# One stage for gate products and memory attention over blocks of 256 tokens, with gating, division and splitting moved to the output stage

## The chip, the core and the metric

The kernel runs on one core of a Trainium2 chip. The metric is the time of the device in microseconds (us), the median of several executions. One further execution was recorded by the hardware profiler; all rows shown here come from it. The engines are TensorE (PE: products, with PEld its weight loads), VectorE (DVE), ScalarE (ACT), GpSimd (POOL) and SyncE (SP), which in this kernel issues every DMA on one queue. Each engine works through its own instructions in order, and they meet at semaphores.

## The reference

Two request groups of 2048 and 512 tokens (2560 rows of width 1024) go through two layers with the same weights. Layer 0 mixes by latent attention with 12 heads, layer 1 by a spatial gating MLP. Both have a memory attention beside it and a gate on top. Cut to what the change touches:

```
q = rmsnorm(q_mem.reshape(S, 4, 64), mq_g)               # q_mem, gate: columns of h @ w_in
s = einsum('qhd,khd->hqk', q, k) * 64 ** -0.5            # k, v: 256 memory rows
o_mem = einsum('hqk,khd->qhd', softmax(s), v)            # 256 columns
o = concatenate([o_mix, o_mem]) * silu(gate)             # o_mix: 768 columns
x = x + o @ w_out[i]
```

All in float32. The kernel keeps that precision by splitting each factor into a high part and a low part and by making three products (hi x hi, hi x lo, lo x hi) of each.

## The kernel before

The program is a sequence of stages. Each has its own buffers and semaphores (`Space`) and ends in a barrier of all engines: `latents`, `heads`, `attention`, then for each layer (`spatial` first in layer 1) `memory_keys` (names mk_), `memory_attention` (ma_), `gating` (ga_) and `output` (ou_). Between stages data lies in DRAM: `hT` (normed input, transposed and split, 1 MB for each of 20 tiles of 128 tokens), `omix` (o_mix and o_mem, transposed), `sums` and `inv_s` (softmax sums of the 12 heads and their reciprocals, since layer 0's o_mix isn't divided yet), `ogT` (gated o, transposed and split).

**Weights.** A `Plan` lists the tiles of a stage's weights. One raw buffer of 6144 columns is shared by all stages; as many tiles as fit (8 at most) are loaded in the stage before (`load_following`, line 137), after that stage has split its own. ACT rounds each tile to its high part (`round_hi`, line 149), DVE takes the low part (`take_lo`, line 154), SP loads the others as slots come free (`load_rest`, line 131). PE waits for single tiles (`ready`).

**attention.** SP loads q of chunk 0, K of head 0, q of chunk 1, V of head 0, q of chunk 2, then K and V of head 1, and then `row(c0)` (line 1006): four small copies of the negated maxima of chunk 0 into a row of q, without which PE can't make the first scores (line 1077). They wait for `neg_in`, which DVE raises after the maxima of all of head 0's keys.

**memory_attention** (line 1432) goes through 20 tiles of 128 tokens with each engine's order staggered over four tiles. For one tile: PE makes q (24 products of 256 columns), ACT squares it, DVE sums over heads, POOL raises the mean to -1/2, DVE scales, PE turns q, ACT and DVE round and split it, PE makes scores (6 products of 512 columns), DVE takes the maximum and its scaled negative `ntop`, ACT makes four exponentials with their sums, DVE divides, PE turns p (8 transposes), ACT and DVE round and split, PE makes the values (16 products of 128 columns), ACT and DVE add the two halves, SP stores to `omix`.

**gating** (line 1668) goes through 5 blocks of 512 tokens by 8 groups of 128 gate columns, 24 products of 512 columns each (960 in all), four PSUM buffers deep. ACT takes silu, DVE divides o (layer 0: the first 6 of the 8 groups, by `inv_s`), multiplies, ACT and DVE split, SP stores `ogT` in two DMAs a group, and loads h, o and the reciprocals. In layer 0 DVE first adds the two rows of `sums` and takes the reciprocal (lines 1800 and 1802).

**output** (line 1828) goes through 20 tiles: load o, split already (1 MB), 48 products of 512 columns, DVE adds x (line 1899), SP stores. ACT does nothing but round the weights. With the last tiles of a stage SP has already fetched the next stage's weights: in layer 0 those are the spatial stage's, 4 x 0.75 MB.

Of the kernel before, what the change touches and what calls it, by code (L numbers as in the profile page):

```python
# [12 lines left out]
P = 128  # L13
# [915 lines left out]
def attention(nc, K, qT, kT, vS, omix, sums_out):  # L929
# [4 lines left out]
    with Space(nc, "at") as s:  # L934
# [52 lines left out]
        with nc.Block() as block:  # L987

            @block.sync
            def _(sp):  # L990
# [441 lines left out]
def memory_attention(nc, K, plan, following, g_q, hT, M, omix, name):  # L1432


    SC = float(MHD) ** -0.5
    with Space(nc, name) as s:
        w = Weights(s, plan, following)
        h = s.sb("h", [P, 2, 2, D], F32R)
# [11 lines left out]
        e = s.sb("e", [P, MH, MEM])  # L1450
        pn = s.sb("pn", [P, 2, MH, MEM])
        p_hi = s.sb("p_hi", [P, MH * 2, P], F32R)
        p_lo = s.sb("p_lo", [P, MH * 2, P], F32R)
        up = s.sb("up", [MHD, MH * P])
        ost = s.sb("ost", [MHD, 2, MH * P])
        q_ps = s.ps("q", [P, MW])
        t_ps = s.ps("t", [P, 2, P])
        s_ps = s.ps("s", [P, MH, MEM])
        p_ps = s.ps("p", [P, MH * 2, P])
        o_ps = s.ps("o", [P, MH * P])  # L1460
        (g_in, mm, squared, red, mean_in, rstd_in, normed, turned, qh, ql, scored, top_in, ntop_in, exps,
         inv_in, pn_in, p_turned, ph, plo, valued, up_in, o_in) = (s.sem(n) for n in (
             "g_in", "mm", "squared", "red", "mean_in", "rstd_in", "normed", "turned", "qh", "ql", "scored",
             "top_in", "ntop_in", "exps", "inv_in", "pn_in", "p_turned", "ph", "plo", "valued", "up_in",
             "o_in"))
        h_in = [s.sem(f"h{u}") for u in range(2)]
        o_out = [s.sem(f"o_out{u}") for u in range(2)]
        with nc.Block() as block:

            @block.sync  # L1470
            def _(sp):
                sp.dma_start(g[:], g_q).then_inc(g_in, 16)
                for u in range(2):
                    sp.dma_start(f32(h[:, u]), hT[u]).then_inc(h_in[u], 16)
                w.load(sp)

                def step(j, u):
                    t, t2, t3 = Tile(j, u), Tile(j, u, 2), Tile(j, u, -3)
                    if t2.within(TILES):
                        sp.wait_ge(mm, t.n + 1)  # L1480
                        sp.dma_start(f32(h[:, u]), hT[bass.ds(t2.n, 1)].rearrange("o p a n -> (o p) a n")
                                     ).then_inc(h_in[u], 16)
                    if t3.within(TILES):
                        sp.wait_ge(o_in, t3.n + 1)
                        sp.dma_start(omix[MIX:MIX + MW, bass.ds(t3.n * P, P)].rearrange(
                            "(h d) t -> d h t", h=MH),
                            ost[:, t3.slot, :].rearrange("d (h t) -> d h t", h=MH)
                            ).then_inc(o_out[t3.slot], 16)

                run_tiles(sp, 3, step, 3)  # L1490
                for u in range(2):
                    sp.wait_ge(o_out[u], 16 * TILES // 2)

            @block.tensor
            def _(pe):
                def q_of(t):
                    pe.wait_ge(h_in[t.slot], t.half * 16 + 16)
                    after(pe, normed, t.n)
                    for k in range(KD):
                        if t.known and t.n == 0:  # L1500
                            w.ready(pe, "q", k)
                        ks = slice(k * P, (k + 1) * P)
                        m = product(pe, q_ps[:], h[:, t.slot, 0, ks], h[:, t.slot, 1, ks],
                                    w.hi["q"][:, k], w.lo["q"][:, k], k == 0, k == KD - 1)
                    m.then_inc(mm, 1)
# [40 lines left out]
                def step(j, u):  # L1546
                    for what, t in ((turn_p, Tile(j, u, -3)), (turn_q, Tile(j, u, -1)),
                                    (q_of, Tile(j, u)), (values, Tile(j, u, -3)),
                                    (scores, Tile(j, u, -1))):
                        if t.within(TILES):  # L1550
                            what(t)
# [692 lines left out]
```

## Time and profile before

| | us |
|---|---|
| median of 3 executions (lowest, highest) | 3594.59 (3593.68, 3597.07) |
| the profiled execution | 3603.56 |
| its span, first to last instruction | 3601.5 |

| engine | busy us | share of the span |
|---|---|---|
| PE | 3326.9 | 92% |
| PEld | 2735.6 | 76% |
| DVE | 2006.2 | 56% |
| ACT | 1581.8 | 44% |
| POOL | 1389.1 | 39% |

The mean granted clock of TensorE is 0.951 of full speed.

| stretch of the span | stage |
|---|---|
| 497 to 1746 | attention |
| 1746 to 1787 | memory_keys, layer 0 |
| 1787 to 1963 | memory_attention, layer 0 |
| 1963 to 2208 | gating, layer 0 |
| 2208 to 2437 | output, layer 0 |
| 2437 to 2910 | spatial |
| 2910 to 2951 | memory_keys, layer 1 |
| 2951 to 3371 | memory_attention and gating, layer 1 |
| 3371 to 3601 | output, layer 1 |

Some durations of single instructions that occur again after the change, from the groups by line: silu of 128x512 0.60, DVE's subtraction of 128x1024 1.22, its addition from PSUM of 128x1024 1.23, ACT's rounding of 128x1024 1.04, addition and reciprocal of the sums 0.40 and 1.65, table load of ACT 1.28.

How to read the rows: each instruction has a start, a duration, an engine, a line, and names of what it writes and reads. What stands in brackets is the time that its engine stood idle before it, and who ended that. A row of PE gives the latency of a product; consecutive products overlap, so what a run of them costs is the distance of starts. A row of SP gives the time that issuing took. Rows with "x4" are several instructions in one.

### The profile page before, as it was taken

Reading aid. Unit: us, or ns where it says so; the run is one execution under the profiler, and the core shown is the slowest. Engines: PE = TensorE matmul, PEld = TensorE weight load, DVE = VectorE, ACT = ScalarE, POOL = GpSimd, SP = SyncE. Lnnn points to the kernel's source line nnn. Section 1 sums busy time; section 2 is a strip of 40 time slices with the busy share of each in tenths; the row PEclk is TensorE's granted clock in tenths of the full one; section 3 lists DMA queues with packets and bytes.
Section 4 is the critical chain, followed back from the end, with each engine's and each line's share of the span. In section 5 each row is a group of like instructions: output and inputs, shape, how many; then the busy total and the mean of one; then the engine's idle time right before and its main releaser. Section 6 shows DMA issues by size and latency. Waiting matters only on the chain. (4 is left out here: it accounts for less than half of the span.)

```text
span 3601.5 us, 46116 instructions
## 1 busy us (share of the span) xinstructions
PE 3326.9 (92%) x16108; PEld 2735.6 (76%) x16108; DVE 2006.2 (56%) x3007; ACT 1581.8 (44%) x2396; POOL 1389.1 (39%) x914
## 2 busy tenths in 40 slices
PE   8969959999999999999697998997999959799899
PEld 8968837777777777777496887885888849688787
DVE  4457758888888888888376332113333337522211
ACT  4446627777777777777454121003222225412100
POOL 1148828888888888888410000000000011000000
PEclk9979969999999999999898999998999969799999
DMA  7769980222222221221354996554222244488555
GB/s 279 260 225 314 306 233 18 66 67 61 67 62 65 52 56 44 67 61 22 115 174 129 290 292 217 197 175 177 88 91 103 90 180 165 131 259 242 175 189 173
DMA packets 454870, 537.91 MB, mean 149 GB/s; under 512 B 55609, under 2 KB 372409, under 8 KB 434993
## 3 DMA queue, kind: packets, MB, share of 16 engines
q1 hardware_dynamic: 454704, 535.81, 48.5%
q8 instruction: 92, 1.51, 0.2%
q14 instruction: 74, 0.60, 0.1%
HBM read 324.98 MB, written 210.61 MB: 149 GB/s over the span
## 5 line engine op out<-in xcount | busy, mean ns | idle before, releaser
L1235 POOL TENSOR_TENSOR at_acc<-at_acc,at_ph 128x1024 f32<-128x1024 f32 x288 | 690.9, 2399 | 79.0 <-ACT at_ph L1161 58.2
L1269 DVE TENSOR_TENSOR at_pl<-at_sc,at_ph 128x1024 fp32r<-128x1024 f32 x408 | 498.6, 1222 | 139.3 <-ACT at_sc L1162 139.0
L1161 ACT ACTIVATE at_ph<-at_sc 128x1024 fp32r<-128x1024 f32 x408 | 418.5, 1026 | 336.2 <-PE at_sc L1081 336.1
L1255 DVE TENSOR_REDUCE at_mx<-at_mxp 128x1 f32<-128x512 f32 x816 | 522.2, 681 | 26.7 <-PE at_mxp L1092 25.0
L1162 ACT ACTIVATE at_sc<-at_sc 128x1024 f32<-128x1024 f32 x408 | 416.3, 1020 | 0.0
L1077 PE MATMUL at_sc<-at_qt,at_kt 97*128 97x512 f32 x816 | 331.4, 406 | 12.5 <-DMA at_qt<-at_neg 9.7
L1079 PE MATMUL at_sc<-at_qt,at_kt 96*128 96x512 f32 x816 | 326.0, 399 | 0.0
L1106 PE MATMUL at_o_hi<-at_ph,at_v 128*128 128x512 f32 x816 | 322.4, 395 | 2.1 <-DVE at_half L1274 2.1
L1081 PE MATMUL at_sc<-at_qt,at_kt 96*128 96x512 f32 x816 | 323.7, 397 | 0.0
L1108 PE MATMUL at_o_lo<-at_pl,at_v 128*97 128x512 f32 x816 | 321.8, 394 | 0.0
L1092 PE MATMUL at_mxp<-at_kt,at_qt 96*128 96x512 f32 x816 | 276.8, 412 | 25.2 <-DMA at_kt<-kT 20.4
L165 PE MATMUL ga_acc<-ga_h,ga_g_hi 128*128 128x512 f32 x640 | 256.1, 400 | 28.4 <-DMA ga_h<-hT 27.6
L165 PE MATMUL ou_acc<-ou_o_hi,ou_o 128*128 128x512 f32 x640 | 250.8, 392 | 26.2 <-DMA ou_o<-ogT 26.2
L1899 DVE TENSOR_TENSOR ou_y<-ou_acc,ou_x 128x1024 f32<-128x1024 f32 x40 | 49.0, 1225 | 380.9 <-PE ou_acc L167 380.9
L166 PE MATMUL ga_acc<-ga_h,ga_g_hi 128*128 128x512 f32 x640 | 253.4, 396 | 0.0
L167 PE MATMUL ga_acc<-ga_h,ga_g_lo 128*128 128x512 f32 x640 | 253.3, 396 | 0.0
L166 PE MATMUL ou_acc<-ou_o_lo,ou_o 128*128 128x512 f32 x640 | 250.5, 391 | 0.0
L167 PE MATMUL ou_acc<-ou_o_hi,ou_o 128*128 128x512 f32 x640 | 250.2, 391 | 0.0
L1092 PEld LDWEIGHTS at_mxp<-at_kt,at_qt 96*128 96x128 f32 x816 | 156.3, 192 | 91.5 <-DVE at_mx L1255 33.0
L253 POOL TENSOR_TENSOR sg_n_mse<-sg_n_ms,all_eps 128x1 f32<-128x1 f32 x24 | 5.0, 209 | 560.0 <-ACT sg_n_junk L245 560.0
L1077 PEld LDWEIGHTS at_sc<-at_qt,at_kt 97*128 97x128 f32 x816 | 154.5, 189 | 75.6 <-DVE at_pl L1269 26.8
L165 PE MATMUL sg_acc<-sg_uv_hi,sg_n_h 128*128 128x512 f32 x480 | 194.6, 406 | 1.8 <-ACT sg_uv L2022 1.2
(246 smaller groups left out, 7350.5 us busy)
## 6 DMA issues: line engine op xcount, KB each, us to landing
ma_h<-hT SPq DMA_DIRECT2D x40, 1024.0 KB, 4.8
ogT<-ga_st SPq DMA_DIRECT2D x160, 256.0 KB, 3.5
ou_o<-ogT SPq DMA_DIRECT2D x40, 1024.0 KB, 6.1
ga_h<-hT SPq DMA_DIRECT2D x64, 512.0 KB, 7.3
hT<-lat_n_h SPq DMA_DIRECT2D x24, 1024.0 KB, 6.2
hT<-sg_n_h SPq DMA_DIRECT2D x24, 1024.0 KB, 3.8
qT<-hd_stq SPq DMA_DIRECT2D x60, 384.0 KB, 6.2
kT<-hd_stk SPq DMA_DIRECT2D x120, 192.0 KB, 3.5
```

Of the source, the lines that this page charges most:

```text
L165: pe.matmul(out, a_hi, w_hi, start=first, stop=False)
L166: pe.matmul(out, a_hi, w_lo, start=False, stop=False)
L167: return pe.matmul(out, a_lo, w_hi, start=False, stop=last)
L1077: pe.matmul(sc[g][:, b, :], kt[:, c.kv, 0, ks], qt[:, c.quad, 0, :], start=True, stop=False)
L1079: pe.matmul(sc[g][:, b, :], kt[0:QK, c.kv, 0, ks], qt[0:QK, c.quad, 1, :], start=False, stop=False)
L1081: m = pe.matmul(sc[g][:, b, :], kt[0:QK, c.kv, 1, ks], qt[0:QK, c.quad, 0, :], start=False, stop=True)
L1092: pe.matmul(mxp[n % 2][:], qt[0:QK, c.quad, 0, qn * P:(qn + 1) * P], kt[0:QK, c.kv, 0, kb * BLK:(kb + 1) * BLK], start=True, stop=True).th ...
L1161: act.activation(ph[:, g], sc[g % 2][:], ACT.Exp, scale=SCALE).then_inc(p_hi, 1)
L1162: act.activation(sc[g % 2][:], sc[g % 2][:], ACT.Exp, scale=SCALE).then_inc(p_in, 1)
L1235: pool.tensor_tensor(acc[:, c.slot, :], f32(ph[:, (g - 1) % 4]).rearrange("p b n -> p (b n)") if t == 1 else acc[:, c.slot, :], now, ALU.a ...
L1255: dve.tensor_reduce(mx[:, n:n + 1], mxp[n % 2][:], AX.X, ALU.max).then_inc(mx_in, 1)
L1269: dve.tensor_tensor(pl[:, g], sc[g % 2][:], f32(ph[:, g]), ALU.subtract).then_inc(p_lo, 1)
```

## The change

- `memory_attention` and `gating` become one stage, `gate_memory` (names gm). It goes through 10 blocks of 256 tokens. For each of the two tiles of a block the steps of memory attention are made as before (two exponential buffers, no buffer for divided p), and the 8 groups of gate products, now 256 columns wide, stand between them in an order written out by hand. The values are made for both tiles at once, 16 products of 256 columns. ACT takes silu of two groups at a time (128x512, four a block), and SP stores it to a new array `sgT` in one DMA. Loops are unrolled.
- h is loaded by blocks (2 MB), two buffers deep, once; gating's own loading of h is gone, and so are its loading of o and its storing of `ogT`.
- Weights: q's eight tiles are laid into two of 128x1024 (`Spaced`), with gate's eight in one plan of ten. Six fit in the raw buffer and are fetched in `memory_keys`.
- In layer 0 the sums are loaded after h of blocks 0 and 1; DVE adds and inverts them ahead of its first norm.
- `gated_output` loads `omix`, `sgT` and, in layer 0, the reciprocals repeated to 64 partitions, in pieces of 128 tokens (512 bytes); DVE divides (768 columns) and multiplies (1024), ACT rounds, DVE takes the low part, PE multiplies with the weights as before. The first tile's steps stand ahead of the rounding and splitting of weights on ACT and DVE, and DVE prepares tile i + 1 ahead of the addition of tile i.
- In `attention` `row(c0)` moves ahead of the loads of chunk 2's q and of head 1's K and V.

The diff, cut to its core:

```diff
@@ attention, sync
                 load_v(0)
+                sp.wait_ge(const_in, 5)
+                row(c0)
                 load_q(c0.ahead(2))
                 load_k(1)
                 load_v(1)
-                sp.wait_ge(const_in, 5)
-                row(c0)
@@ gate_memory (was memory_attention and gating)
+                load_h(0)
+                w.load_rest(sp)
+                load_h(1)
+                if sums is not None:
+                    sp.dma_start(rows[:], flat).then_inc(rows_in, 16)
+                w.load_following(sp)
...
+                def step(b):                       # tensor
+                    i = TB * b
+                    q_of(i)
+                    gates(b, 0)
+                    turn_q(i)
+                    q_of(i + 1)
+                    scores(i)
+                    gates(b, 1)
+                    turn_q(i + 1)
+                    gates(b, 2)
+                    scores(i + 1)
+                    turn_p(i)
+                    gates(b, 3)
+                    gates(b, 4)
+                    turn_p(i + 1)
+                    gates(b, 5)
+                    values(b, 0)
+                    gates(b, 6)
+                    values(b, 1)
+                    gates(b, 7)
...
+                def exp(i):                        # scalar
+                    act.wait_ge(ntop_in, i + 1)
+                    after(act, p_turned, i - 1)
+                    after(act, inv_in, i)
...
+                def step(b):                       # scalar
+                    i = TB * b
+                    square(i)
+                    q_round(i)
+                    square(i + 1)
+                    exp(i)
+                    silu(b, 0)
+                    q_round(i + 1)
+                    p_round(i)
+                    exp(i + 1)
+                    silu(b, 1)
+                    p_round(i + 1)
+                    silu(b, 2)
+                    upper(b, 0)
+                    upper(b, 1)
+                    silu(b, 3)
...
+                def step(b):                       # vector
+                    i = TB * b
+                    norm(i)
+                    norm_scale(i)
+                    q_low(i)
+                    norm(i + 1)
+                    maximum(i)
+                    norm_scale(i + 1)
+                    divide(i)
+                    q_low(i + 1)
+                    maximum(i + 1)
+                    p_low(i)
+                    divide(i + 1)
+                    p_low(i + 1)
+                    halves(b, 0)
+                    halves(b, 1)
@@ gated_output (was output), sync
-                sp.dma_start(f32(o[:, 0]), ogT[0]).then_inc(o_in[0], 16)
+                load_o(0)
                 w.load_rest(sp)
-                sp.dma_start(f32(o[:, 1]), ogT[1]).then_inc(o_in[1], 16)
+                load_o(1)
                 for u in range(2):
                     sp.dma_start(x[:, u, :], rows_of(u)).then_inc(x_in[u], 16)
                 w.load_following(sp)
+                for i in range(TILES):
+                    u = i % 2
+                    if i + 2 < TILES:
+                        sp.wait_ge(mixed, i + 1)
+                        load_o(i + 2)
@@ gated_output, scalar and vector
+                round_og(0)
                 w.round_hi(act)
+                for i in range(1, TILES):
+                    round_og(i)
...
+                gated(0)
+                low(0)
+                w.take_lo(dve)
+                for i in range(TILES):
+                    if i + 1 < TILES:
+                        gated(i + 1)
+                        low(i + 1)
+                    add(i)
@@ build
-                      Plan(raw, [("q", k_tiles(w_in, q0, q0 + MW), MW)]),
-                      Plan(raw, [("g", k_tiles(w_in, q0 + MW, q0 + MW + D), D)]),
+                      Plan(raw, [("q", Spaced(w_in, q0).rows, D),
+                                 ("g", k_tiles(w_in, q0 + MW, q0 + MW + D), D)]),
```

Step names: `gates(b, f)` is one group of 24 gate products (G0 to G7), `turn_q`, `scores`, `turn_p`, `values` are PE's steps of memory attention for tile i, `divide` and `halves` DVE's.

## Rows read from the trace of the kernel before

**Rows 1.** Busy time by stretch: us, each engine's busy time, PEclk, DMA share, GB/s.
```profile
1787.40:1963.20 175.80, 153.73 (x1120) 144.98 (x1120) 119.75 (x268) 84.84 (x249) 20.14 (x20) 0.91 0.43 153
1963.20:2207.70 244.50, 226.10 (x960) 182.93 (x960) 82.86 (x120) 54.48 (x89) 0.00 (x0) 0.95 0.93 266
2020.00:2100.00 80.00, 80.00 (x354) 66.25 (x353) 29.35 (x45) 18.16 (x32) 0.00 (x0) 1.00 1.04 295
2951.10:3371.50 420.40, 380.87 (x2080) 328.96 (x2080) 181.02 (x356) 139.91 (x339) 20.14 (x20) 0.93 0.66 199
```

**Rows 2.** Timeline of PE, one tile of memory attention: start us, us, engine, line, operation.
```profile
1903.46 0.23 PE L1540 MATMUL ma_o<-ma_p_hi,mem_mv 128*128 128x128 f32 x1
...
1905.20 0.45 PE L165 MATMUL ma_s<-mem_mk_hi,ma_qT_hi 128*128 128x512 f32 x1
...
1906.65 1.04 PE L1529 MATMUL ma_p<-all_ident,ma_pn 128*128 128x128 f32 x8
...
1907.53 0.38 PE L1511 MATMUL ma_t<-all_ident,ma_qn 128*128 128x128 f32 x2
...
1907.66 0.36 PE L165 MATMUL ma_q<-ma_q_hi,ma_h 128*128 128x256 f32 x1
...
1910.61 0.23 PE L1540 MATMUL ma_o<-ma_p_hi,mem_mv 128*128 128x128 f32 x1
```

**Rows 3.** Timeline at the start of attention, and four copies later (603.16).
```profile
499.66 13.46 SPq L992 DMA_DIRECT2D at_qt<-qT  x1
...
520.87 11.10 SPq L1009 DMA_DIRECT2D at_qt<-at_neg  x4
...
534.18 0.80 PE L1077 MATMUL at_sc<-at_qt,at_kt 97*128 97x512 f32 x1 [9.74 <-DMA at_qt<-at_neg]
...
603.16 2.42 SPq L1009 DMA_DIRECT2D at_qt<-at_neg  x4
```

**Rows 4.** Timeline of the first tile of memory attention: q's square and its turning.
```profile
1797.67 0.38 ACT L1589 ACTIVATE ma_sq<-ma_q 128x256 f32<-128x256 f32 x1 [7.67 <-PE ma_q L167]
...
1800.39 0.69 PE L1511 MATMUL ma_t<-all_ident,ma_qn 128*128 128x128 f32 x2 [2.81 <-DVE ma_qn L1646]
```

**Rows 5.** Timeline of ACT and DVE in a steady tile of memory attention.
```profile
1900.17 1.21 DVE L1613 TENSOR_REDUCE ma_top<-ma_s 128x4 f32<-128x1024 f32 x1
...
1900.57 1.01 ACT L1572 CAST ma_p_hi<-ma_p 128x1024 fp32r<-128x1024 f32 x1 [1.75 <-PE ma_p L1529]
...
1901.85 0.48 ACT L1583 ACTIVATE ma_e<-ma_s,ma_ntop 128x256 f32<-128x256 f32 x1
...
1903.66 0.40 ACT L1589 ACTIVATE ma_sq<-ma_q 128x256 f32<-128x256 f32 x1
...
1904.03 1.14 DVE L1633 TENSOR_SCALAR ma_pn<-ma_e,ma_inv 128x256 f32<-128x256 f32 x4
```

**Rows 6.** Timeline of layer 1 where its first exponential needs another table.
```profile
2972.57 1.28 ACT L1583 ACT_TABLE_LOAD   x1
...
2972.71 0.17 DVE L1616 TENSOR_SCALAR ma_ntop<-ma_top 128x4 f32<-128x4 f32 x1
...
2973.86 0.47 ACT L1583 ACTIVATE ma_e<-ma_s,ma_ntop 128x256 f32<-128x256 f32 x1
```

**Rows 7.** Timeline at the starts of memory attention, gating, output and memory_keys.
```profile
1759.10 0.33 SPq L1334 DMA_DIRECT2D mk_h<-hT  x1
...
1792.72 0.58 PE L165 MATMUL ma_q<-ma_q_hi,ma_h 128*128 128x256 f32 x1 [9.39 <-DMA ma_h<-hT]
...
1964.26 6.90 DVE L154 TENSOR_TENSOR ga_g_lo<-all_w_raw,ga_g_hi 128x1024 fp32r<-128x1024 f32 x6 [4.56 <-ACT ga_g_hi L149]
...
2212.77 0.80 PE L165 MATMUL ou_acc<-ou_o_hi,ou_o 128*128 128x512 f32 x1 [13.10 <-DMA ou_o<-ogT]
```

**Rows 8.** Timeline at the end of gating.
```profile
2201.00 1.46 DVE L1807 TENSOR_TENSOR ga_st<-ga_og,ga_st 128x512 fp32r<-128x512 f32 x2
```

**Rows 9.** DMA issues of attention's V: KB each, median us to landing.
```profile
at_v<-vS SPq DMA_DIRECT2D x12, 1280.0 KB, 7.8
```

More of the change, by code:

```diff
@@ new lines, in q_of, with gates @@
+                    m.then_inc(q_mm, 1)
+                def gates(b, f):
+                    m = b * PAIRS + f // 2
+                    if f % 2 == 0:
+                        after(pe, sg_in, m - 1)
+                    fs = slice(f * P, (f + 1) * P)
+                    for k in range(KD):
+                        if b == 0 and f == 0:
+                            w.ready(pe, "g", k)
+                        ks = slice(k * P, (k + 1) * P)
+                        last = product(pe, gate[m % 2][:, f % 2, :], w.hi["g"][:, k, fs], w.lo["g"][:, k, fs],
+                                       h[:, b % 2, :, 0, ks], h[:, b % 2, :, 1, ks], k == 0, k == KD - 1)
+                    if f % 2 == 1:
+                        last.then_inc(gate_mm, 1)
@@ L1546, in step, with values @@
[L1546 to L1551, printed above, removed]
-                run_tiles(pe, 3, step, 3)
+                def values(b, half):
+                    group = TB * b // PT_TILES
+                    if half == 0:
+                        pe.wait_ge(plo, TB * (b + 1))
+                    after(pe, o_in, 2 * b + half)
+                    for n in range(2 * half, 2 * half + 2):
+                        out = ot[:, (n % 2) * W:(n % 2 + 1) * W]
+                        for c in range(2):
+                            vt = M.v[:, group, c, n].rearrange("p a d -> p (a d)")
+                            pe.matmul(out, vt, p_hi[:, 2 * n + c, :], start=c == 0, stop=False)
+                            m = pe.matmul(out, vt, p_lo[:, 2 * n + c, :], start=False, stop=c == 1)
+                    m.then_inc(valued, 1)
@@ L1867, in _ @@
             def _(pe):
-                def step(j, u, first, last):
-                    i = j * 2 + u
-                    pe.wait_ge(o_in[u], j * 16 + 16)
-                    if not first:
-                        pe.wait_ge(y_in, i - 1)
+                for i in range(TILES):
+                    u = i % 2
+                    pe.wait_ge(lo_in, i + 1)
+                    after(pe, y_in, i - 1)
                     for k in range(KD):
-                        if first and u == 0:
+                        if i == 0:
                             w.ready(pe, "o", k)
@@ L1890, in _, with gated @@
             def _(dve):
[L1891 to L1894 removed]
+                def gated(i):
+                    u = i % 2
+                    dve.wait_ge(o_in[u], LOADS * (i // 2 + 1))
+                    if inv_s is not None:
+                        dve.tensor_tensor(o[:, u, 0:DIV], o[:, u, 0:DIV], r[:, u], ALU.mult
+                                          ).then_inc(divided, 1)
+                        dve.wait_ge(divided, i + 1)
+                    after(dve, lo_in, i)
+                    dve.tensor_tensor(full[:], o[:, u].rearrange("p k t -> p (k t)"),
+                                      sg[:, u].rearrange("p k t -> p (k t)"), ALU.mult).then_inc(mixed, 1)
```

498 lines of the change are left out of this document (194 added, 304 removed).

## The prediction

> **What bounds the kernel now.** I read four views in this order: the engines' busy shares and the slices of the page, busy time by stretch, the order of instructions in time inside each stage that the diff touches, and the groups by line. TensorE is busy 92% of the span. In the middle of a stage it never stops: 80 us of gating hold 80.00 us of PE and 354 products at the full clock, 0.226 us each [rows 1]. What is left over sits at the ends of stages, where the engine waits and its granted clock falls: memory attention plus gating take 420.3 us in the first layer and 420.4 us in the second, at a granted clock of 0.91 to 0.95 [rows 1].
>
> Inside them the steady part is small. One tile of memory attention lasts 7.16 us: q 2.95, values 1.74, scores 1.45, turning p 0.88, turning q 0.13 [rows 2]. Twenty tiles are 143 us, and 960 gate products at 0.2266 are 217.5 us, together 360.7. So 59.6 us per layer are start, drain and barriers of two stages, which one stage can partly save.
>
> **The sum is made against the profiled execution**, 3603.56 us with a span of 3601.5. It lies 9.0 us above the median 3594.59, and I take 9.0 off at the end.
>
> **Part 1: attention's first row.** SP's fifth load is held 13.46 us at issue, behind the queue's earlier loads [rows 3]. The next K and V go out behind it, and then the four small copies of the maxima take 11.10 us to issue, where the same four take 2.42 us in a quiet queue; PE waits 9.74 us for them until 534.18 [rows 3]. After the change nothing is issued between the first V load and these copies. They start at 520.87 as before, since the maxima come no earlier, and are there at about 520.9 + 1.8 + 2.0 = 524.7. Gain 9.4. The second K and V then load beside chunk 0 and are used a head later; the third q a chunk later. Bounds: 5 (the queue is still half full) and 9.7.
>
> **Part 2: the joint stage, per block of two tiles.** PE's work, each from rows 2: q 48 products x 0.1195 = 5.7; scores 2.9; turning p 1.8; turning q 0.3. The gate product is now 256 columns wide. q's 256-column products take (2.95 - 0.08)/24 = 0.1195 us, and 512 columns take 0.2266, so halving costs 0.0124 us each: 192 x 0.1195 = 22.9 for what took 96 x 0.2266 = 21.8. The values go the other way, 16 products of 256 columns, 1.9, for 32 of 128 columns, 3.5. With about 0.8 for the changes of kind the sum is 36.3 us; before, two tiles took 14.3 + 21.8 = 36.1. The work itself is a tie.
>
> Then the waits. From q's end to q's turning the chain ACT, DVE, POOL, DVE takes 2.8 us [rows 4]; one gate group (24 x 0.1195 = 2.9) covers it, leaving 0.1. The second tile's chain is covered by scores and a group, 4.3.
> The long chain begins at q_of(i+1)'s end, set to 0. Scores end at 1.45, the maximum (1.21) and its scaling at 3.1 [rows 5]. Four exponentials, 1.81 [rows 5], end at 5.05. ACT must then change its table: the load is 1.28 us [rows 6]. Silu (0.60, like the other single durations without a group from the short list beside the tables of time and profile) ends at 6.95, q's rounding at 7.4, its low part at 7.95. PE reaches scores(i+1) at 7.45, so it stalls 0.5. Later, counted from that point C: p turned at 2.3, rounded (1.01) at 3.55, table load, exponentials at 6.65, divided (1.14 for four) at 8.05; PE arrives at turn_p(i+1) at 8.1. No stall. The rest, G5 to G7 and the two halves of the values, has gate groups of 2.9 between steps of 1.4. Block: 36.3 + 0.1 + 0.5 = about 36.8 (7.95 + 28.8 by the same walk). Ten blocks: 368, 7.3 more than the 360.7.
>
> Four table loads a block, 80 in all, are 103 us of ACT, but ACT needs only some 16 us of 36.8. The load before exp(i) costs nothing if it runs ahead of the wait: in layer 1 it began 0.14 us before the ntop scaling had even started, and the exponential followed at once (2972.57 + 1.28 = 2973.85, started 2973.86) [rows 6]. That instruction had one wait; here exp has three, so a load could stand behind the first of them (a rival below).
> The Trainium skill speaks against this part. Its page "ScalarE: Activation LUTs", section "What ACT_TABLE_LOAD costs", gives 1283 ns for the load and about 1380 ns of drain, 2.66 us a switch, and the section on table sets tells one to batch calls by set. The load's figure is in the trace; the drain isn't. By the row the block is 36.8, by the page about 39.5.
>
> **Start of the joint stage.** T is the barrier's end (1787.4). Before, q's first product started at T + 5.3, after 1 MB of h [rows 7]. Now the block's 2.1 MB must be in: at about 0.30 MB/us (295 GB/s in rows 1) and 1.5 to 2 latency, T + 9. Four of ten weight tiles (2.1 MB) follow h: the last at T + 15.5, rounded at 16.5 and split at 17.8 (DVE 1.15 a tile, from six in 6.90) [rows 7]. ACT and DVE take all ten before the first square, so turn_q(0) starts at T + 20. In layer 0 DVE also waits for the sums, which SP issues behind the second block's 2.1 MB: T + 23.3, then the addition and the reciprocal (0.40 and 1.65), turn_q(0) at T + 27.7. From there the rest of block 0 is 30.9 + 2 for the low clock, nine blocks are 331.2, silu to barrier 5.7 (DVE's last split ended at 2202.5, the next stage began at 2207.7) [rows 1, 8]. Layer 0: 397.5; layer 1: 389.8. Gain 22.8 and 30.6.
>
> **The stage before it.** memory_keys now fetches 6 x 0.5 MB ahead, not 8 x 0.125, and its third h goes out at 1759.10 [rows 7] behind what is left of them, about 1 MB: + 3.5 us per layer (0 to 5).
>
> **The output stage.** PE's products are unchanged, 48 x 0.2266 = 10.9 a tile. New per tile: DVE 0.95 + 1.22 + 1.22 beside the addition's 1.23 (128x1024), 4.6; ACT 1.0. Both fit. SP issues four more loads, 0.6 each as in the quiet queue [rows 3]. DMA: layer 0 reads 2816 pieces of 512 B. V's load is 2560 pieces of 512 B, landing in 7.8 us [rows 9]; less 2 latency that is 2.3 ns a piece. By gating's 295 GB/s it is 1.7. So 4.9 to 6.4 us, and 3.3 for x and y: 8 to 9.7 of 10.9. It just fits.
> The start doesn't. PE began 5.1 us after the barrier [rows 7], since the weights' split needs no data of the stage. Now the first split stands on DVE behind gated(0) and low(0), and ACT's rounding behind round_og(0): load 7.5, product 0.95 + 1.22, rounding 1.0, low 1.22, first split 1.2: PE at 13.3 in layer 0, + 8.2; in layer 1, with fewer pieces and no division, + 6.2. In layer 0 load_o(1) waits for two splits, which costs tile 1 about 2.5, and load_o(2) is queued behind the 3.1 MB of the spatial stage's weights: about 40.8 against the 35 at which tile 2 would need it, some 6 to 9 more (0 to 9). Output: + 19 in layer 0, + 6.5 in layer 1.
>
> **Sum.** Attention - 9.4; layer 0: - 22.8 + 3.5 + 19 = - 0.3; layer 1: - 30.6 + 3.5 + 6.5 = - 20.6. Together - 30.3: 3573.3 profiled, **3564.5 as a median**. Nearly all of the gain is in attention and in layer 1.
>
> **Rivals.**
> (a) The table load stands behind exp's first wait. Then exp(i) starts 1.3 later and so does scores(i+1): block 38.1, + 1.3 x 20 = 26: 3591. For: three waits. Against: the load that the trace shows ran ahead of its one.
> (b) A switch holds ACT for two loads' time, 2.57: scores(i+1) at 9.3 and turn_p(i+1) 1.2 late, block 39.3, + 2.5 x 20 = 50: 3615, slower. It decides from about 1.9 us a switch. Against: 0.01 us between load and exponential [rows 6]. This is the direction in which the skill's page above would take it.
> (c) Slower: the output stage becomes DMA-bound. The reads are columns of two arrays and rows repeated to 64 partitions. It decides where a piece costs over 2.7 ns (2816 x 2.7 + 3.3 = 10.9); at 3.5 ns a tile of layer 0 takes 13.1, 20 tiles + 44: 3609. For: V's 2.3 is near, and no repeated row of this size is in the trace. Against: gating moved 295 GB/s in such pieces.
> (d) More gain: the starts overlap better (keys + 0, no late load_o): 3548.
>
> **How the numbers follow.** Forecast 3564.5 within 12 us: 0.50; (d) 0.13; (a) 0.20; (b) 0.05; (c) 0.12. The 8-in-10 range reaches down to (d) with more of the first row's bounds and up past (a): 3540 to 3600. A measurement of this kernel can tell about 0.2%, 7.2 us. Faster by over that (below 3587.4): the forecast, (d) and a small part of (a), 0.66; within it: most of (a), 0.18; slower: (b), (c), 0.16.
>
> **What would show it.** Right: PE's first score product in attention near 525; blocks of 36.8 us in the joint stage with a stall of about 0.5 us before the second tile's scores and table loads directly after the previous ACT instruction; turn_q(0) 20 and 28 us after the barriers; PE in output starting 13 and 11 us after the barrier, then 10.9 us a tile. Wrong: blocks of 38 or more (then see where the load stands against exp's waits, and what lies between load and function), output tiles over 11 us that wait on DMA, or PE idle between later blocks, which would mean that an ordering of ACT or DVE which I walked through once does not repeat.

## The result, and the profile after

| | before | after |
|---|---|---|
| median of 4 executions (lowest, highest), us | 3595.83 (3593.68, 3597.61) | 3546.10 (3543.66, 3553.82) |
| span of the profiled execution, us | 3601.5 | 3546.5 |
| mean granted clock | 0.951 | 0.963 |

The ratio is 0.9864, 95% interval 0.9851 to 0.9877: by the medians the changed kernel is 49.7 us faster. Forecast was 30.3 less than before, 3564.5 us, with 3540 to 3600 as the range. The two traced executions lie further apart than the medians, 55.0 us, because that of before was 7.8 us above its median and that of after 2.3.

By stretch, in the columns of rows 1; the stretches are attention, memory_keys, the joint stage and output of layer 0, then 100 us from the middle of the joint stage, then the joint stage and output of layer 1:

```profile
494.53:1730.09 1235.56, 1208.06 (x5016) 919.46 (x5016) 1065.35 (x1409) 888.74 (x997) 1057.92 (x529) 0.98 0.25 58
1730.09:1775.13 45.04, 27.21 (x104) 21.18 (x104) 15.87 (x40) 12.64 (x32) 7.59 (x6) 0.80 0.44 163
1775.13:2163.22 388.09, 364.97 (x2880) 354.64 (x2880) 135.16 (x272) 170.49 (x329) 20.14 (x20) 0.97 0.30 103
2163.22:2412.25 249.03, 222.56 (x960) 182.92 (x960) 101.50 (x88) 28.78 (x28) 0.00 (x0) 0.95 0.77 216
1900.00:2000.00 100.00, 99.07 (x790) 96.34 (x790) 33.20 (x71) 43.78 (x88) 6.04 (x6) 1.00 0.29 98
2928.72:3309.96 381.24, 364.62 (x2880) 354.29 (x2880) 133.14 (x270) 171.78 (x330) 20.14 (x20) 0.98 0.30 104
3309.96:3546.40 236.44, 220.63 (x960) 181.83 (x960) 81.12 (x68) 28.79 (x28) 0.00 (x0) 0.96 0.62 182
```

The joint stage stands for two stages of before, 420.3 us together [rows 1]. Its clock is 0.97, theirs was 0.91 and 0.95. Stage by stage, in us:

| | before | after | difference | forecast |
|---|---|---|---|---|
| start to attention | 497.1 | 494.5 | -2.6 | 0 |
| attention | 1249.3 | 1235.6 | -13.7 | -9.4 |
| memory_keys, layers 0 and 1 | 41.1, 41.2 | 45.0, 43.4 | +4.0, +2.2 | +3.5, +3.5 |
| joint stage, layer 0 | 420.3 | 388.1 | -32.2 | -22.8 |
| output, layer 0 | 229.5 | 249.0 | +19.5 | +19 |
| spatial | 472.7 | 473.1 | +0.4 | 0 |
| joint stage, layer 1 | 420.3 | 381.2 | -39.1 | -30.6 |
| output, layer 1 | 230.0 | 236.5 | +6.5 | +6.5 |
| sum | | | -55.0 | -30.3 |

The code ahead of attention is the same in all kernels here, and it ends anywhere from 493.2 to 499.8 us in their traces; its 2.6 us are no effect of the change. Single stages scatter too. memory_keys took 40.7 to 41.5 us in the three traces that have it with memory attention and gating behind it (before and two experiments), and 42.6 to 47.9 us in the nine with the joint stage behind it and memory_keys as in the changed kernel. Their means are 44.2 in layer 0 and 44.8 in layer 1, so the +4.0 and +2.2 of the table stand for about +3.1 and +3.5. In the table's trace PE waits once for its third h, 2.97 us in layer 0 (line below) and 1.79 in layer 1; before it did not wait there.

**Attention's start.** The timeline of SP and PE after the change, which answers rows 3:

```profile
517.94 2.52 SPq L1009 DMA_DIRECT2D at_qt<-at_neg  x4
...
521.92 0.80 PE L1077 MATMUL at_sc<-at_qt,at_kt 97*128 97x512 f32 x1 [0.41 <-DMA at_qt<-at_neg]
...
523.37 0.63 PE L1077 MATMUL at_sc<-at_qt,at_kt 97*128 97x512 f32 x1
...
528.94 0.40 PE L1077 MATMUL at_sc<-at_qt,at_kt 97*128 97x512 f32 x1
```

The four copies take 2.52 us to issue instead of 11.10, and PE waits 0.41 us for them instead of 9.74. From the stage's first load to the first score it takes 27.4 us instead of 37.1. The scores run at 0.63 us until 526 and at 0.40 afterwards. The 0.63 us is not an effect of the wait alone: in both kernels the pairs of products for the maxima, which come before it, already took 1.39 us each, where later ones take 0.62.

**A block of the joint stage.** ACT, DVE and PE around the second tile's scores, answering rows 5 and 6:

```profile
1841.02 1.28 ACT L1667 ACT_TABLE_LOAD   x1
...
1843.27 0.17 DVE L1741 TENSOR_SCALAR gm_ntop<-gm_top 128x4 f32<-128x4 f32 x1
...
1843.47 0.47 ACT L1667 ACTIVATE gm_e<-gm_s,gm_ntop 128x256 f32<-128x256 f32 x1 [1.17 <-DVE gm_ntop L1741]
...
1845.42 1.28 ACT L1679 ACT_TABLE_LOAD   x1
...
1846.72 0.60 ACT L1679 ACTIVATE gm_sg<-gm_gate 128x512 f32<-128x512 f32 x1
...
1847.21 0.47 ACT L1660 ACTIVATE gm_qT_hi<-gm_ot,gm_g 128x256 fp32r<-128x256 f32 x1
...
1847.71 0.48 DVE L1733 SCALAR_TENSOR_TENSOR gm_qT_lo<-gm_ot,gm_g,gm_qT_hi 128x256 fp32r<-128x256 f32 x1 [0.92 <-ACT gm_qT_hi L1660]
...
1848.25 0.50 PE L165 MATMUL gm_s<-mem_mk_hi,gm_qT_hi 128*128 128x512 f32 x1 [0.31 <-DVE gm_qT_lo L1733]
```

Exp's table is loaded at 1841.02, 2.25 us before its `ntop` begins, and ACT then idles 1.17 us with the table in place. Silu starts 0.02 us after its load ends (1845.42 + 1.28 = 1846.70). The chain silu, rounding of q, low part ends last, and PE waits for it once a block. This is the path that the forecast walked. The distance of blocks is 36.39 to 36.42 us for all nine pairs in each layer. The groups by line count the loads of the stage, 79 in both layers together:

```profile
L1679 ACT ACT_TABLE_LOAD x40 | 51.3, 1283 | 0.7
L1667 ACT ACT_TABLE_LOAD x39 | 50.0, 1283 | 0.7
```

**The starts** of memory_keys and the joint stage (barrier T at 1775.13), and of the joint stage of layer 1 (T at 2928.72), by the timeline:

```profile
1750.97 0.50 PE L165 MATMUL mk_acc<-mk_kv_hi,mk_h 128*128 128x512 f32 x1 [2.97 <-DMA mk_h<-hT]
...
1782.23 0.49 SPq L1524 DMA_DIRECT2D gm_rows<-sums  x1
...
1794.78 0.41 DVE L1711 TENSOR_TENSOR gm_rows<-gm_rows 128x240 f32<-128x240 f32 x1 [3.36 <-DMA gm_rows<-sums]
...
1798.95 0.69 PE L1582 MATMUL gm_ot<-all_ident,gm_qn 128*128 128x128 f32 x2 [6.85 <-DVE gm_qn L1726]
...
2946.14 0.44 PE L1582 MATMUL gm_ot<-all_ident,gm_qn 128*128 128x128 f32 x2 [1.45 <-DVE gm_qn L1726]
```

Turning q(0) starts at T + 23.8 in layer 0, where DVE waited for the sums until 1794.78, and at T + 17.4 in layer 1.

**The output stage** (barriers at 2163.22 and 3309.96):

```profile
2171.13 0.96 DVE L1869 TENSOR_TENSOR ou_o<-ou_o,ou_r 128x768 f32<-128x768 f32 x1 [13.34 <-DMA ou_r<-inv_s]
...
2176.97 0.77 PE L165 MATMUL ou_acc<-ou_o_hi,ou_og 128*128 128x512 f32 x1 [17.65 <-DVE ou_o_lo L154]
...
2194.92 0.50 PE L165 MATMUL ou_acc<-ou_o_hi,ou_og 128*128 128x512 f32 x1 [4.34 <-DVE ou_og L1878]
...
2211.25 0.50 PE L165 MATMUL ou_acc<-ou_o_hi,ou_og 128*128 128x512 f32 x1 [3.52 <-DVE ou_og L1878]
...
3320.41 0.76 PE L165 MATMUL ou_acc<-ou_o_hi,ou_og 128*128 128x512 f32 x1 [14.30 <-DVE ou_o_lo L154]
```

PE starts 13.75 and 10.45 us after the barriers, where it was 5.1 before [rows 7]. Tiles 1 and 2 of layer 0 come late by 4.3 and 3.5 us, and then PE waits for nothing more in layer 0.

### The profile page after: what moved, and what is told of

It reads as the page before. It is cut to its first block and busy times, and to the rows that moved or that the text cites. A ratio compares the mean times of both kernels' runs of the same rounds, so it can differ in the third digit from the quotient of the medians.

```text
span 3546.5 us, 48006 instructions
## 1 busy us (share of the span) xinstructions
PE 3295.6 (93%) x17708; PEld 2787.6 (79%) x17708; DVE 2005.1 (57%) x2905; ACT 1686.6 (48%) x2420; POOL 1390.3 (39%) x914
## 5 line engine op out<-in xcount | busy, mean ns | idle before, releaser
L1255 DVE TENSOR_REDUCE at_mx<-at_mxp 128x1 f32<-128x512 f32 x816 | 521.7, 680 | 24.7 <-PE at_mxp L1092 23.1
L165 PE MATMUL gm_gate<-gm_h,gm_g_hi 128*128 128x256 f32 x1280 | 367.3, 287 | 1.8 <-DVE gm_g_lo L154 1.8
L166 PE MATMUL gm_gate<-gm_h,gm_g_hi 128*128 128x256 f32 x1280 | 362.1, 283 | 0.0
L167 PE MATMUL gm_gate<-gm_h,gm_g_lo 128*128 128x256 f32 x1280 | 362.0, 283 | 0.0
L1644 POOL TENSOR_TENSOR gm_rstd<-gm_mean,all_mhalf 128x4 f32<-128x4 f32 x40 | 40.3, 1007 | 681.3 <-DVE gm_mean L1721 681.3
L165 PE MATMUL ou_acc<-ou_o_hi,ou_og 128*128 128x512 f32 x640 | 252.3, 394 | 40.0 <-DVE ou_o_lo L154 32.0
L166 PE MATMUL ou_acc<-ou_o_lo,ou_og 128*128 128x512 f32 x640 | 251.8, 393 | 0.0
L167 PE MATMUL ou_acc<-ou_o_hi,ou_og 128*128 128x512 f32 x640 | 251.6, 393 | 0.0
L165 PEld LDWEIGHTS gm_gate<-gm_h,gm_g_hi 128*128 128x128 f32 x1280 | 244.8, 191 | 3.1 <-DVE gm_g_lo L154 2.2
L166 PEld LDWEIGHTS gm_gate<-gm_h,gm_g_hi 128*128 128x128 f32 x1280 | 245.1, 191 | 0.9
L167 PEld LDWEIGHTS gm_gate<-gm_h,gm_g_lo 128*128 128x128 f32 x1280 | 245.0, 191 | 0.0
```

The source lines that it names most:

```text
L165: pe.matmul(out, a_hi, w_hi, start=first, stop=False)
L166: pe.matmul(out, a_hi, w_lo, start=False, stop=False)
L167: return pe.matmul(out, a_lo, w_hi, start=False, stop=last)
L1255: dve.tensor_reduce(mx[:, n:n + 1], mxp[n % 2][:], AX.X, ALU.max).then_inc(mx_in, 1)
```

## Experiments

The theory after the result: each part does what the forecast said, and the sizes of the joint stage were off. What had to be told apart: whether the table loads are hidden, whether the 36.4 us of a block are work or waits, and what in the starts is late. All ratios are to the kernel before on the same chip; its median there was 3599.1 with the first four kernels, 3598.6 with the next four and 3598.2 with the last three. Differences to the changed kernel's 3546.1 cross these groups and are uncertain by some 8 us, so the stages of the traces are given beside them. "After" is the changed kernel.

**The row alone.** Before, with the two lines of the row moved:

```
+                sp.wait_ge(const_in, 5)
+                row(c0)
                 load_q(c0.ahead(2))
                 load_k(1)
                 load_v(1)
-                sp.wait_ge(const_in, 5)
-                row(c0)
```

> The kernel before with one edit: attention's row(c0) ahead of the loads of chunk 2's q and of head 1's K and V. Theory (the copies stood behind the V load in the queue, and TensorE's granted clock stayed low after the wait): attention shortens by 12 to 13 us, the first score product comes 9.7 us sooner after the stage's start, and the time is 3583. Rival (the row was worth only its wait, and the other 4 us of attention's gain came from something else in the change): 9.4 us, 3586.5.

3588.7 us, ratio 0.9972 (0.9962 to 0.9982): 10.1 us faster by the ratio, interval 6.5 to 13.7. The times allow both gains that were expected; the rival's, 9.3 below the 3595.8 of before, is nearer. The timeline of this kernel:

```profile
518.91 2.52 SPq L1009 DMA_DIRECT2D at_qt<-at_neg  x4
...
522.88 0.80 PE L1077 MATMUL at_sc<-at_qt,at_kt 97*128 97x512 f32 x1 [0.40 <-DMA at_qt<-at_neg]
```

**All but the row.** After, with the order of before in attention (the reverse of the diff above).

> The changed kernel with attention's order as before. Theory (the parts add up): 3546 + 12.5 = 3558.5. Rival (the row's move is worth less or more beside the others): outside 3554 to 3563.

3559.2 us, ratio 0.9888 (0.9871 to 0.9904). The wait is back:

```profile
522.96 9.77 SPq L1009 DMA_DIRECT2D at_qt<-at_neg  x4
...
536.01 0.79 PE L1077 MATMUL at_sc<-at_qt,at_kt 97*128 97x512 f32 x1 [9.48 <-DMA at_qt<-at_neg]
...
543.03 0.40 PE L1077 MATMUL at_sc<-at_qt,at_kt 97*128 97x512 f32 x1
```

The two parts add up within their intervals: by the ratios 40.3 us for the rest and 10.1 for the row, against 48.9 for both. The whole of attention took 1249.3, 1247.4 and 1244.2 us in the three traces with the old order (before, the split gates and this one) and 1235.1 to 1237.5 in ten traces with the new one. The means are 1247.0 and 1236.1: the row is worth 10.9, and the 13.7 of the first pair holds some 3 us of chance. Part of that chance is the clock. The kernel before, which waited 9.74 us, still ran scores at 0.63 us in this row:

```profile
546.11 0.63 PE L1081 MATMUL at_sc<-at_qt,at_kt 96*128 96x512 f32 x1
```

That is 11.9 us after its first score. The last such score came 8.5 us after the first in the kernel with gate products in halves (wait of 10.39 us), 4.9 us in this one (9.48 us), and 3.6 and 4.0 us in the two above that waited 0.4 us. Why the first stayed low for longest isn't settled.

**No table loads.** After, with silu replaced by a function that needs no other table. The product with the gate is then another function of it.

```
-  act.activation(sg[:, m % 2, :], gate[m % 2][:].rearrange("p f t -> p (f t)"), ACT.Silu
+  act.activation(sg[:, m % 2, :], gate[m % 2][:].rearrange("p f t -> p (f t)"), ACT.Square
```

> The changed kernel with Square in the place of Silu in gate_memory, a function for which no table has to be changed; silu is left out of what is computed. 80 table loads of 1.28 us, 103 us of ScalarE, are gone. Theory (they are hidden but for 0.3 us a block, where q's rounding of the second tile waits behind load and silu): 20 x 0.3 = 6 us less, 3540. Rival (a switch costs more than its load, or ScalarE sets the block): 25 us or more less, below 3521.

3533.9 us, ratio 0.9828 (0.9811 to 0.9844), 12.2 us below the changed kernel's median (13 by the ratios): twice what the theory had, half of the rival's least. The new function takes as long as silu, 0.60 us. Blocks went from 36.41 to 35.62 us (from one block's first q product to the next, 1873.86 to 1910.27 and 1871.62 to 1907.24). Below are 100 us of its stage and its second turning of p, where 0.12 us is the distance of products that wait for nothing:

```profile
1900.00:2000.00 100.00, 100.00 (x808) 98.22 (x807) 34.62 (x76) 30.80 (x81) 6.05 (x6) 1.00 0.29 100
```

```profile
1889.84 0.28 PE L167 MATMUL gm_gate<-gm_h,gm_g_lo 128*128 128x256 f32 x1
...
1889.96 1.03 PE L1600 MATMUL gm_p<-all_ident,gm_e 128*128 128x128 f32 x8
...
1890.76 0.36 PE L165 MATMUL gm_gate<-gm_h,gm_g_hi 128*128 128x256 f32 x1
```

In the changed kernel the same three rows are

```profile
1892.66 0.28 PE L167 MATMUL gm_gate<-gm_h,gm_g_lo 128*128 128x256 f32 x1
...
1892.92 1.09 PE L1600 MATMUL gm_p<-all_ident,gm_e 128*128 128x128 f32 x8
...
1893.77 0.36 PE L165 MATMUL gm_gate<-gm_h,gm_g_hi 128*128 128x256 f32 x1
```

So 79 loads of 1.28 us, 101 us of ACT, cost 12 or 13 us by the times and 15 by the blocks. They cost it in two places per block: 0.58 us between the last gate product and the second tile's first score product instead of 0.12, and 0.34 instead of 0.23 from that product to the next, 0.57 together; and 0.26 + 0.85 us around the second turning of p instead of 0.12 + 0.80, 0.19. Together 0.76.

**Gate products in halves.** Before, with each gating product of 512 columns made as two of 256:

```
-                    for k in range(KD):
+                    for c in range(2):
+                        cs = slice(c * BLK // 2, (c + 1) * BLK // 2)
+                        for k in range(KD):
...
-                        m = product(pe, acc[n % 4][:], w.hi["g"][:, k, fs], w.lo["g"][:, k, fs],
+                            m = product(pe, acc[n % 4][:, cs], w.hi["g"][:, k, fs], w.lo["g"][:, k, fs],
```

> The kernel before with each gate product of 512 columns made as two of 256, group by group, all k for one half and then for the other. 1920 more products in all. Theory (a product costs its columns and a fixed 0.0124 us): 1920 x 0.0124 = 24 us more, 3620. Rival (the width is free, and the changed kernel's blocks were short for another reason): within 5 us of 3596.

3627.9 us, ratio 1.0081 (1.0065 to 1.0098): 29 us slower (23 to 35), where 24 were expected; in its trace memory attention and gating together are 13.8 us longer in layer 0 and 15.0 in layer 1. The stretch of rows 1, in this kernel:

```profile
2020.00:2100.00 80.00, 80.00 (x669) 80.00 (x668) 26.57 (x41) 17.03 (x30) 0.00 (x0) 1.00 1.01 285
```

80 / 669 = 0.1196 us a product; the forecast had taken 0.1195 from the q products. Two of them are 0.239 where one of 512 columns is 0.226: 0.013 us each, 960 x 0.013 = 12.5 us a layer. So the narrower products cost what was expected. That the 0.013 us is a fixed cost of each product is not shown: by that rule 128 columns would take 0.066 us, and they take 1.74 / 16 = 0.109 [rows 2].

**Two switches more, at two places.** After, with two tiny activations (silu, exp) and so two more table loads a block, ahead of the first silu or ahead of the fourth:

```
+                def switches(b):
+                    for n, f in enumerate((ACT.Silu, ACT.Exp)):
+                        after(act, tiny_in, 2 * b + n)
+                        act.activation(tiny[:, n:n + 1], K.ones[:, 0:1], f).then_inc(tiny_in, 1)
...
+                    switches(b)
                     silu(b, 0)
```

> The changed kernel with two more table switches in each block, ahead of silu(b, 0): one Silu and one Exp of 128x1 into a spare tile, nothing else changed. Two loads and two small functions, about 3.1 us of ScalarE. Theory (this is the one place of the block where ScalarE is on TensorE's path): the block grows by 3.1, 20 x 3.1 = 62 us, 3608. Rival (ScalarE is busy only 16 of 36 us, so 3 more are covered): within 10 us of 3546.

> The same two small functions and two more table loads a block, but ahead of silu(b, 3), where ScalarE waits 2.3 us for the gate products and again 2.3 us before the next square. Theory: covered, 3546 within 8 us. Rival (each switch costs TensorE its own time wherever it stands, or drains more than it shows): 3596 or more.

Ahead of the first: 3637.2 us, ratio 1.0106 (1.0085 to 1.0128), 91 us above the changed kernel (87 by the ratios). Ahead of the fourth: 3550.1 us, 0.9864 (0.9843 to 0.9886); that this is the changed kernel's ratio to the last digit is chance, but its blocks take the same 36.4 us. The same 100 us in the kernel with them ahead of the fourth; ACT is busy 53.44 instead of 43.78, and PE is unmoved:

```profile
1900.00:2000.00 100.00, 99.05 (x789) 96.09 (x788) 33.87 (x75) 53.44 (x102) 6.05 (x6) 1.00 0.28 98
```

The other kernel, by its timeline in two neighbouring blocks and by the same stretch:

```profile
1855.57 0.50 PE L165 MATMUL gm_s<-mem_mk_hi,gm_qT_hi 128*128 128x512 f32 x1 [3.34 <-DVE gm_qT_lo L1741]
...
1857.08 1.88 PE L1602 MATMUL gm_p<-all_ident,gm_e 128*128 128x128 f32 x8
...
1896.42 0.50 PE L165 MATMUL gm_s<-mem_mk_hi,gm_qT_hi 128*128 128x512 f32 x1 [3.35 <-DVE gm_qT_lo L1741]
...
1897.93 1.03 PE L1602 MATMUL gm_p<-all_ident,gm_e 128*128 128x128 f32 x8
```

```profile
1900.00:2000.00 100.00, 93.31 (x730) 90.41 (x729) 29.44 (x61) 46.83 (x89) 4.04 (x4) 0.97 0.23 78
```

The wait grows by 3.03 us, the two loads and their two tiny functions. Blocks grow by 4.4 (40.84 instead of 36.4). I had expected 62 us more and got 91, because after a wait of 3.34 us the granted clock falls: in the first of the two blocks the eight transposes of p have a latency of 1.88 instead of 1.03 us, and the products behind them run at half speed until 1860.46. That is the other 1.4 us a block. It does not follow every time. In the second of the two blocks the wait is the same, the clock stays, and the block takes 39.46 us, 3.05 more than 36.41, which is the growth of the wait. Of the 18 distances of blocks in this trace two are of this kind, the others are 40.8 us or more. A load is free where ACT has slack, and costs more than its length where it is on the path.

**The output stage.** Two versions of after. In the first version the next stage's weights are fetched from tile 3 on, not ahead of tile 2:

```
-                w.load_following(sp)
                 for i in range(TILES):
...
+                    if i == 3:
+                        w.load_following(sp)
```

In the second also six weight tiles are rounded and split ahead of tile 0's gating, and `load_o(1)` goes out ahead of the stage's own last weights:

```
                 load_o(0)
-                w.load_rest(sp)
                 load_o(1)
+                w.load_rest(sp)
...
+                w.round_hi(act, 0, 6)
                 round_og(0)
-                w.round_hi(act)
+                w.round_hi(act, 6)
...
+                w.take_lo(dve, 0, 6)
                 gated(0)
                 low(0)
-                w.take_lo(dve)
+                w.take_lo(dve, 6)
```

> The changed kernel with the output stage's fetch of the next stage's weights (3.1 MB in layer 0) moved from ahead of tile 2's loads to behind tile 5's. Theory (tile 2's loads stand behind these weights in the queue, 3.52 us of wait, and the restart): 4 us less, 3542. Rival (tile 2 is late because its own pieces of 512 bytes are slow): 3546, and tile 2 still waits over 2 us.

> out_following, and in the output stage six of eight weight tiles are rounded and split ahead of tile 0's gating, tile 1's loads go out right behind tile 0's. Theory (the first split stands behind the data, and tile 1 behind all the splits): TensorE starts 1 us sooner in each layer, tile 1 isn't late in layer 0 (4.34 us), together with the above 10 to 12 us less than the changed kernel, 3535. Rival (the loads' bandwidth sets the start, so the order only moves the wait): less than 5 us beyond out_following.

The first: 3551.9 us (3545.6 to 3555.2), ratio 0.9867 (0.9849 to 0.9884), no difference that the times can tell. In its trace output of layer 0 takes 245.8 us, not 249.0, and tile 2's wait of 3.52 us is gone while tile 1's stays. The second: 3537.8 us, ratio 0.9828 (0.981 to 0.9846), 8.3 us below the changed kernel's median (13 by the ratios); the trace of the output stages is the surer measure here. Output of layer 0 takes 242.0 us, 7.1 less, and in layer 1 236.5, the same as after. Its starts:

```profile
2174.27 0.96 DVE L1871 TENSOR_TENSOR ou_o<-ou_o,ou_r 128x768 f32<-128x768 f32 x1 [2.09 <-DMA ou_r<-inv_s]
...
2178.88 0.80 PE L165 MATMUL ou_acc<-ou_o_hi,ou_og 128*128 128x512 f32 x1 [18.60 <-DVE ou_og L1880]
...
3315.78 0.80 PE L165 MATMUL ou_acc<-ou_o_hi,ou_og 128*128 128x512 f32 x1 [15.37 <-DVE ou_og L1880]
```

PE starts at T + 14.7 (T = 2164.18), later than the 13.75 of after, because tile 0's data now shares the DMA engines with tile 1's and lands at T + 10.1 instead of T + 7.9. The expected earlier start did not come. But no tile is late afterwards: the gain is the waits of tiles 1 and 2, 7.9 us, less the 0.9 of the later start.

**The swap, and everything together.** After again on the same chip; after with ScalarE's order changed in one place; and a version with all that the above pointed to.

```
                     exp(i)
-                    silu(b, 0)
                     q_round(i + 1)
+                    silu(b, 0)
```

The last one has this swap, the mended output stage (four weight tiles ahead of tile 0, the order of loads as in after), and three edits in the starts: `load_following` of memory_keys behind its last h; the sums fetched ahead of the second block's h, and added and inverted behind the first tile's low part of q; the first square ahead of ACT's last weight tile.

> The changed kernel as it is, beside the two others on one chip, so that their differences to it need no second chip. Expected: 3546 us (3540 to 3554), as in its first timing.

> The changed kernel with one swap in ScalarE's order per block: the rounding of the second tile's q stands ahead of the first silu instead of behind it. Nothing is added or removed, and the table loads stay as they are. Theory: the 0.76 us that a block is longer than the block without table loads all hangs on the one wait of 0.31 us of PE before scores(i+1), which ends with the low part of q, and that one with the rounding behind silu(b,0). With the swap the wait is gone and the block takes 35.6 instead of 36.4 us: 20 x 0.76 = 15 us less than the changed kernel, 3531. Rival: the other 0.45 us of the 0.76 come from ScalarE being slower elsewhere in the block (its groups freed later by the table loads), and only the 0.31 idle goes: 6 us less, 3540, with blocks of 36.1.

> The changed kernel with five orders mended: the next stage's weights fetched behind memory_keys' last h (6 us in both layers), the sums fetched ahead of the second block's h and added after the first q's low part (3 us in layer 0), the rounding of the second q ahead of silu(b,0) (15 us), the first square ahead of the last weight tile's rounding (1 us a layer), and in the output stage four weight tiles rounded and split ahead of the first tile's gating, with the next stage's weights fetched from tile 3 on (7 to 10 us in layer 0, 0 to 2 in layer 1). Sum by the theory: 3546 - 6 - 3 - 15 - 2 - 9 = 3511. Rival: these gains overlap other waits of the same starts, and only the swap's 15 us and the output's 7 are real: 3524.

After again: 3551.1 us, ratio 0.987 (0.9855 to 0.9885). The swap: 3539.0 us, 0.9839 (0.9826 to 0.9852), 12.1 less. Its block is 35.85 us (1871.98 to 1907.83), 0.56 less, between the two theories and explained by neither alone: the whole of the first place goes, the stall with its restart (0.57), and the second place stays. PE and ACT there:

```profile
1843.98 0.49 ACT L1660 ACTIVATE gm_qT_hi<-gm_ot,gm_g 128x256 fp32r<-128x256 f32 x1
...
1844.48 1.28 ACT L1679 ACT_TABLE_LOAD   x1
...
1845.78 0.60 ACT L1679 ACTIVATE gm_sg<-gm_gate 128x512 f32<-128x512 f32 x1
...
1846.48 0.39 PE L165 MATMUL gm_s<-mem_mk_hi,gm_qT_hi 128*128 128x512 f32 x1
```

All together: **3517.5 us (3514.2 to 3520.1), ratio 0.9775 (0.9761 to 0.9788)**, 80.7 us below before and 33.6 below after, where 3511 was expected. That sum had counted 35 from a median of 3546; on this chip the changed kernel stood at 3551.1, so the gain itself came out as expected. By its trace, memory_keys and the joint stage of layer 0 give 16.2 us (3.4 in memory_keys; turning q(0) at T + 18.6 instead of T + 23.8; 5.7 by the swap; most of the remaining 1.9 fits the second tile's q, which runs at 0.28 us from 1795.04 on, where in the changed kernel it ran at 0.41 us from 1799.65 to 1803.07), output of layer 0 7.9, and layer 1 from memory_keys to the end 7.7, where I had counted on 12. Layer 1's part is 1.8 in memory_keys, 4.6 in the joint stage and 1.3 in output. The joint stage has the swap's 5.7, but q(0) is turned at T + 18.6, 1.1 us later than in the changed kernel: PE's first product there waits for h until T + 8.9 instead of T + 7.9. That this comes from fetching the weights later is likely and not tested.

## Why the prediction was right and where it was off

The direction, the path and the parts were right; the forecast time was 18.4 us above the one measured. In the traces the difference to the forecast is 24.7 us. The joint stages of both layers are 9.4 and 8.5 us of it, 17.9 together, and attention and what stands ahead of it 6.9, mostly chance; the rest cancels. The step from the traces to the medians gives 6.7 back, since 9.0 us were taken off for it and the traced execution of the changed kernel lay only 2.3 above its median. (The forecast's own sum gives 3564.3, not 3564.5; nothing hangs on it.)

- **Attention, -9.4.** Right. The copies started 2.9 us earlier than forecast (517.94 against 520.87, of which 2.6 is the earlier start of the stage), and the first score came 9.7 us earlier within the stage. Over thirteen traces the part is 10.9, by the times 10.1.
- **The block, 36.8.** Measured 36.4, and the agreement is better than its terms, which is luck. The stall was forecast 0.5, and the distance of starts there is 0.46 over the normal one. That exp's load runs ahead of its waits, and that a load costs 1.28 and no more, were right. But the work was forecast 36.3, and with no loads the block is 35.6: the 0.8 us "for the changes of kind" hardly exist. Against it, the restart after the stall (0.11) and the second turning of p (0.19) were put at nothing. The walk had p(i+1) ready at 8.05 against PE's arrival at 8.1 us, a margin of 0.05, and such a margin is no cover. Nine blocks from q to q are 3.6 us a layer too many, and what is left of block 0 behind its first turning 0.3 and 0.7.
- **The joint stage's start, T + 27.7 and T + 20.** Measured T + 23.8 and T + 17.4. The chain was right (sums, addition, reciprocal, norm), the rate was not. I took gating's 295 GB/s. Two blocks of h and four weight tiles, 6.3 MB, stood ahead of the sums, which were there at T + 19.65. Less the 2.0 us that a small load takes (the median of the maxima's copies from issue to landing) that is 0.36 MB/us, an estimate. The rate of a stage in which the DMA keeps pace with PE was taken for what the queue can carry. 3.9 and 2.6 us too many.
- **From the last block's work to the barrier, 5.7.** From PE's last product it is 4.1 and 4.0 us, of which 3.3 and 3.2 stand behind the end of silu. The 5.7 came from a stage that ends with a division, two splits and two stores [rows 8]; this one ends with silu and its store. 1.6 and 1.7 us too many. With the two terms above this makes up the 9.4 and 8.5 us.
- **memory_keys, +3.5 each.** Measured +4.0 and +2.2, within the bounds; over nine traces +3.1 and +3.5.
- **Output, +19 and +6.5.** Measured +19.5 and +6.5. PE at 13.3 and 11.3 was 13.75 and 10.45; tiles 1 and 2 were forecast 2.5 and 6 to 9 late and were 4.3 and 3.5. So the sum is better than its terms, luck again: tile 1 was late for want of its data, which the order of loads in the last versions mends.

The rivals. (a), the load behind exp's first wait, is out: it ran 2.25 us ahead of `ntop`. (b), a switch at the price of two loads, is out: silu starts 0.02 us after its load, and the stall per block is 0.31 us. The Trainium skill, page "ScalarE: Activation LUTs", section "What ACT_TABLE_LOAD costs", gives 1283 ns for the load, which the 79 loads show exactly, and a drain beside it, which none of them shows. (c), an output stage bound by DMA, is out: behind tile 2 PE waits for nothing, at 216 GB/s over the stage. (d) named the time that came, 3548 against 3546.1, but its two conditions did not hold: memory_keys and tiles 1 and 2 of output still pay. What came true is its sense, starts of the joint stage that are 3.9 and 2.6 us shorter than forecast.

## What to carry to other kernels

Joining two stages gains what their ends cost, not what their middles do: here two tiles with their gates took 36.1 us of work before [rows 1, 2] and a block takes 36.4, and nearly all of the joint stage's gain came from starts, ends and the clock that falls with them. Price a table load or any other work of a helper engine by its place in that engine's order: the same two loads cost 0 or some 4.4 us a block. Where a walk through a schedule leaves a margin under 0.1 us, count it as a stall, and look whether two steps of the helper can be swapped; the one swap found here is worth 12 us.

## What the runs showed of the hardware that was not expected

- A short stall costs more than its idle time: PE's 0.31 us of idle are 0.57 us of block time, since the last product before it ends its overlap and the first two behind it restart (0.34 us apart instead of 0.23).
- A stall of 3.34 us lowered the granted clock in 16 of 18 distances of blocks and then cost another 1.4 us or more at half speed; one of 0.31 us doesn't (PEclk 1.00 over 100 us). The fall can come behind the restart: after the wait of 4.34 us in output the first three products took 0.50, 0.39 and 0.40 us, and products of 0.63 us followed from 2196.04 to 2198.60. After waits of 9.7 and 9.5 us the scores stayed slow for 11.9 us in one trace and for 4.9 in another.
- In unbroken runs a product of 512 columns takes 0.226 us, two of 256 take 0.239, and one of 128 takes 0.109 [rows 2], nearly as long as one of 256.
- A small load pays for what stands ahead of it in the queue: the sums, issued right behind the weights and the second block's h, landed 12.5 us after their issue began (1782.23 to 1794.78), and the four copies of a row take 2.5 us to issue in a quiet queue and 9.8 to 11.1 behind a chunk's q and the next head's K and V.
